# The scans of a bidirectional RWKV-7 step: from three inverse slots a chunk to one, with three units in flight

## The reference, cut to what matters

```python
xn = rms_norm(x, norm1_g) * (1.0 + sc1) + sh1
z = xn @ p['w_in']                      # r, k, v, decay and rate factors, gates, conv inputs
for each direction (forward, backward):
    def step(S, inp):
        r_t, w_t, k_t, v_t, a_t, b_t = inp
        sa = einsum('bhvk,bhk->bhv', S, a_t)
        S = S * w_t + sa[..., None] * b_t + v_t[..., None] * k_t
        return S, einsum('bhvk,bhk->bhv', S, r_t)
wkv = ys[0] + ys[1]
ln = (wkv - mean) * rsqrt(var + 64e-5) * lnx_w + lnx_b
x_a = (ln + bonuses) * (sigmoid(gl) @ g2)
out = (gate_a * (x_a @ w_pa) + gate_b * ((cb * conv(cc * ch)) @ w_pb)) @ w_o
x = x + gt1 * out;  x = x + gt2 * (relu(norm(x) @ w_ff1) ** 2 @ w_ff2)
```

## Time and profile before

| What | us |
|---|---|
| median of 3 runs | 2954.09 |
| the profiled execution, whole time | 2959.77 |
| its span | 2958.0 |
| TensorE busy in the span | 2803.4 (95%) |
| first and last `ur` copy of the scans | 1079.7 and 1753.4 |

### The profile page before, as it was taken

How to read it: one execution, slowest core, us unless ns; L and a number is a source line. 1 busy time by engine, 2 the same in 40 slices (tenths; PEclk the granted TensorE clock), 3 DMA queues, 4 the chain that set the end, 5 groups by cost and what they waited for, 6 DMA issues and landing times.

```text
span 2958.0 us, 66020 instructions
## 1 busy us (share of the span) xinstructions
PE 2803.4 (95%) x27766; PEld 2599.9 (88%) x27766; DVE 1459.0 (49%) x2957; ACT 839.9 (28%) x1684; POOL 760.4 (26%) x1005
## 2 busy tenths in 40 slices
PE   4899999999999979999999979999699999999997
PEld 2799999999999957777777769999699999999997
DVE  1364584575575536766666652442633333333333
ACT  3434234244243223333333331211411111111112
POOL 0311111111121124444444533212111111111111
PEclk8899999999999989999999999999899999999998
DMA  7323524524424434344334435212011111111101
GB/s 288 104 90 113 166 84 125 157 85 132 146 80 141 131 124 119 118 125 119 110 117 120 133 120 202 78 58 91 29 43 43 43 42 38 40 43 43 43 28 64
DMA packets 276314, 293.81 MB, mean 99 GB/s; under 512 B 76128, under 2 KB 215776, under 8 KB 275936
## 3 DMA queue, kind: packets, MB, share of 16 engines
q1 hardware_dynamic: 267104, 254.54, 28.2%
q0 software_dynamic: 7200, 28.84, 2.6%
q10 hardware_dynamic: 1760, 6.82, 0.6%
HBM read 198.76 MB, written 91.36 MB: 98 GB/s over the span
## 4 chain that ended last, share of the span: by engine, by line
PE 92%; issue 3%; DVE 2%; DMA 2%; ACT 1%; SPq 1%; POOL 0%; DVEq 0%; ACTq 0%; POOLq 0%
PE gbank L718 25%; PE inv L718 23%; PE bank L718 22%; PE ser L718 17%; PE inv L902 2%; PE bank L891 1%; DMA ring<-in_wblocks 1%; DVE xr L1578 0%; DVE xb L1985 0%; DMA xt_d<-xt_s 0%; SPq L534 0%; SPq L477 0%; POOL wsp L681 0%; DVE gmat L1746 0%; SPq L533 0%
## 5 line engine op out<-in xcount | busy, mean ns | idle before, releaser
L681 POOL TENSOR_TENSOR wsp<-ring,wsp 128x1024 fp32r<-128x1024 f32 x88 | 215.5, 2449 | 850.8 <-ACT wsp L1454 829.9
L718 PE MATMUL gbank<-xn_hi,wsp 128*128 128x384 f32 x1312 | 349.8, 340 | 19.1 <-DVE xn_lo L1942 18.2
L611 POOL TENSOR_TENSOR wsp<-ring,wsp 128x1024 fp32r<-128x1024 f32 x67 | 174.9, 2611 | 746.7 <-ACT wsp L1248 746.7
L718 PE MATMUL bank<-xn_hi,wsp 128*128 128x384 f32 x1312 | 346.9, 339 | 0.4 <-POOL wsp L681 0.4
L718 PE MATMUL inv<-xn_hi,wsp 128*128 128x384 f32 x1312 | 345.2, 338 | 0.0
L718 PEld LDWEIGHTS gbank<-xn_hi,wsp 128*128 128x128 f32 x1312 | 240.2, 189 | 24.0 <-issue 15.9
L718 PEld LDWEIGHTS bank<-xn_hi,wsp 128*128 128x128 f32 x1312 | 239.0, 188 | 2.5 <-POOL wsp L681 0.7
L718 PEld LDWEIGHTS inv<-xn_hi,wsp 128*128 128x128 f32 x1312 | 238.6, 187 | 1.8 <-POOL wsp L611 1.1
L1454 ACT ACTIVATE wsp<-ring 128x1024 fp32r<-128x1024 f32 x88 | 92.7, 1053 | 468.5 <-PE inv L718 391.9
L718 PE MATMUL ser<-xn_hi,wsp 128*128 128x384 f32 x816 | 218.9, 342 | 5.4 <-DVE xr L1578 5.4
L718 PE MATMUL bank<-xn_lo,wsp 128*128 128x384 f32 x656 | 221.3, 337 | 1.4 <-issue 1.4
(11 more groups left out here) (380 smaller groups left out, 5525.7 us busy)
## 6 DMA issues: line engine op xcount, KB each, us to landing
ring<-in_wblocks SPq DMA_DIRECT2D x195, 512.0 KB, 3.6
ub<-op_d SPq DMA_DIRECT2D x144, 256.0 KB, 2.8
op_d<-ar SPq DMA_DIRECT2D x32, 576.0 KB, 5.5
op_d<-bk SPq DMA_DIRECT2D x32, 576.0 KB, 6.2
vb<-v_d SPq DMA_DIRECT2D x144, 64.0 KB, 3.1
xt_d<-xt_s POOLq DMA_DIRECT2D x8, 576.0 KB, 3.2
x_d<-zero SPq DMA_DIRECT2D x8, 576.0 KB, 6.6
v_d<-vn SPq DMA_DIRECT2D x8, 576.0 KB, 6.8
```

Source lines behind the costliest of these rows:

```text
L611: GT(wsp[s % 2][1][:], ring[(N_ADA_RING + s) % RING][:], wsp[s % 2][0][:].bitcast(F32), ALU.subtract).then_inc(S["wsplit_lo"], 1)
L681: nc.gpsimd.tensor_tensor(wsp[b % 2][1][:], ring[(N_MIX0 + b) % RING][:], wsp[b % 2][0][:].bitcast(F32), ALU.subtract).then_inc(S["wl_ok"], 1)
L718: return nc.tensor.matmul(out, lhsT, rhs, start=start, stop=stop)
```

## The change

The scans' loop has one inverse slot a round. Round s holds the units s + 1, s + 2 and s + 3, which are at levels 5, 4 and 3, at the fixed places 0, 1, 2 (`slot`). Each step of a level is issued once for the three: three transpositions, one DVE mask, one GpSimd mask (two where the ring of 7 places wraps), three `left`, one ScalarE copy, three `right`, one DVE sum for two units (two where the ring wraps). Both Gram directions are made four rounds ahead; the transposed operands one round ahead instead of two. On TensorE the groups of one tile shape stand together. Loads go to 7 places, `gmat` to 5, `tok` to 2. The last pair's 16x16 blocks lie elsewhere (`xb`), and their 32 loads move from the dense stage to just behind the first four units' loads.

```diff
-SETS = 4
-LOADS = 6
-TOKS = 3
+SETS = 5
+LOADS = 7
+TOKS = 2
+LATE = LEVELS - FIRST
...
-        def at_level(s, i):
-            return [(s + 1, FIRST + i)] if 0 <= s + 1 < UNITS else []
+        def in_flight(s):
+            return [(v, LEVELS - v + s) for v in range(max(s + 1, 0), min(s + LATE, UNITS - 1) + 1)]
+        def slot(v, s):
+            return v - s - 1
...
# SP
-                        sp.wait_ge(S["g_out"], 32 * (p + 1))
-                        blocks_in(p)
+                        if p + 1 < PAIRS:
+                            sp.wait_ge(S["g_out"], 32 * (p + 1))
+                            blocks_in(p)
...
             pl_load(0)
             pl_load(1)
+            emptied(PAIRS - 1, "zb")
+            sp.wait_ge(S["g_out"], 32 * PAIRS)
+            blocks_in(PAIRS - 1)
             for v in range(4, LOADS):
...
# GpSimd
+            for s in range(-4, UNITS):
+                if in_flight(s):
+                    trimmed(s)
+                if there(s + 3):
+                    start_inverse(s + 3, 0)
+                    start_inverse(s + 3, 1)
+                    start_inverse(s + 3, 2)
+                if there(s + 1):
+                    triangles(s + 1)
...
# TensorE
+            for s in range(-4, UNITS):
+                p, j = divmod(s, NC)
+                inverses, serial, ahead = in_flight(s), there(s), there(s + 4)
+                if inverses:
+                    turn(s)
+                if there(s + 1):
+                    token_major(s + 1)
+                if serial:
+                    ur_state(s)
+                if ahead:
+                    gram(s + 4, 0, (0, 1, 2))
+                if serial:
+                    serial_ur(s)
+                    if j == 4:
+                        pe.wait_ge(S["ada_ok"], p + 1)
+                for x in finals(s - 1):
+                    spread(*x)
+                if inverses:
+                    left(s)
+                if serial:
+                    y_state(s)
+                if ahead:
+                    gram(s + 4, 1, (0, 1))
+                if serial:
+                    serial_u(s)
+                    if j == 2:
+                        modulation(p)
+                if inverses:
+                    right(s)
+                if ahead:
+                    gram(s + 4, 1, (2,))
+                for x in finals(s):
+                    mean(*x)
+                if serial:
+                    serial_s(s)
+                    serial_y(s)
+                    if j == 3:
+                        modulation_turned(p)
+                for x in finals(s):
+                    gate(*x)
+                    variance(*x)
...
# ScalarE, a round: deviation(s-1), y_out(s-1), tokens(s+1), ur_out, product_out, u_out,
#                   (j == 2) mrow, last_blocks(s+1), squares_of(s)
# DVE
+            for s in range(-4, UNITS):
+                p, j = divmod(s, NC)
                 if NC <= s < NC + SUB - 1:
                     substitution(PAIRS - 1, [s - NC])
+                for x in finals(s - 1):
+                    reciprocal(*x)
...
+                if there(s - 1):
+                    y_add(s - 1)
+                if in_flight(s):
+                    turned(s)
+                if there(s):
+                    carried(s)
+                if there(s + 4):
+                    gram(s + 4, 0)
+                for x in finals(s - 1):
+                    scaled(*x)
+                if in_flight(s):
+                    summed(s)
+                for x in finals(s):
+                    centred(*x)
+                if there(s):
+                    states(s)
+                    if j == NC_LAT and p + 1 < PAIRS:
+                        first_state(p + 1)
+                if there(s + 4):
+                    gram(s + 4, 1)
```

More of the change, by code:

```diff
@@ L631, in start_inverse, with trimmed @@
                     GT(lm[v % 2][part - 1][:], ltc[q][:], two(offm[:, part - 1, :]), ALU.mult).then_inc(S[f"lm{FIRST + part - 1}_ok"], 1)
-            def trimmed(s, i):
-                both, n = at_level(s, i), round_of(s, i)
+            def trimmed(s):
+                n = round_of(s)
+                pool.wait_ge(S["xt_ok"], sums(n))
                 if n:
-                    pool.wait_ge(S["xt_ok"], sums(n))
                     pool.wait_ge(S["p1_full"], n)
[L639 to L642, removed]
+                if there(s + LATE):
+                    pool.wait_ge(u_in[(s + LATE) % LOADS], 80 * ((s + LATE) // LOADS + 1))
+                parts = runs([v for v, lev in in_flight(s)])
+                for v, q in parts:
+                    x = slice(slot(v, s), slot(v, s) + q.stop - q.start)
+                    ins = GT(xtb[:, x, :, :], xt[:, q, :, :], trim[:, x, :].unsqueeze(2).to_broadcast([P, q.stop - q.start, 2, HD]), ALU.mult)
+                ins.then_inc(S["xtb_ok"], 1)
             def triangles(v):
@@ L1076, in there @@
                 return 0 <= v < UNITS
-            for s in range(-3, UNITS):
+            for s in range(-4, UNITS):
                 p, j = divmod(s, NC)
[L1080 to L1092, removed]
-                    if inverses:
-                        left(s, i)
-                    if there(s):
-                        (serial_ur, serial_u, serial_s)[i](s)
-                    if i == 0:
-                        if there(s) and j == 4:
-                            pe.wait_ge(S["ada_ok"], p + 1)
-                        for x in finals(s - 1):
-                            spread(*x)
-                    if inverses:
-                        right(s, i)
-                    if i == 0 and there(s + 2):
-                        token_major(s + 2)
-                    if i == 1:
-                        for x in finals(s):
-                            mean(*x)
-                        if there(s + 3):
-                            gram(s + 3, 0, (0, 1))
-                    if i == 2:
-                        if there(s):
-                            serial_y(s)
-                        if there(s) and j == 3:
-                            modulation_turned(p)
-                        for x in finals(s):
-                            gate(*x)
-                            variance(*x)
-                    if there(s) and j == 2 and i == 2:
-                        modulation(p)
```

198 lines of the change are left out of this document (82 added, 116 removed).

## The result

The changed kernel takes 2870.86 us (median of 4 runs, 2867.05 to 2873.18), the kernel before beside it 2956.82 (4 runs): ratio 0.9706, interval 0.9683 to 0.973. The forecast was 2903. The sign and the stage were right; the gain was 86 us instead of 51. Run again later, it gave 0.9739 (0.9715 to 0.9763).

The account below looks back on a forecast made before the run. TensorE's own queue was taken as the bound. Gains of 60 and 12.5 less losses of 10.6, 10.5 and 0.5 gave 51 us off 2959.8; less 5.7 for the median, 2903 us, range 2870 to 2940.

Parts of the forecast that it names:

- ordinary round, 70 times: Scan rounds: six fewer TensorE shape changes and shorter waits inside a level save 0.86 us a round, 60 us in all.
- waits with missing cover: TensorE waits at j = 7, j = 8 and j = 3, of 0.5, 0.5 and 0.6 us, go: 12.5 us won.
- the y add: TensorE waits 0.33 us for VectorE's `y_add` before `ur_state` in 32 rounds: 10.6 us lost.
- last pair's substitution: VectorE's step at the start of rounds 9 to 23 delays `y_add` or a mask: 10.5 us lost, 25 at most.
- last rounds, beyond an ordinary gain: The last four rounds have no Gram at all, which returns about 3 us.
- start: Moved block loads and eight Gram directions with masks before round 0 make the first serial part about 3.5 us later.
- shape is not what costs: Rival, chance 0.12: tile shape on TensorE costs nothing, only waits are gained, 5 us; total 2949.
- The slower rival: Chance 0.08: VectorE's mask of direction 1 holds TensorE 1.5 us late in all 72 rounds; total 3003.
- the price of a shape change: TensorE's queue in the scans: each change of tile shape costs 0.11 us, six fewer save 0.66 a round.
- The second reading in the forecast: By the skill's drain rule, each of six TensorE shape changes is worth 0.12 us, or 0.72 a round.
- The 0.2 for the waits of `left`: TensorE's `left` is held by the mask into `tc`; new cover saves 0.1 us for each of two levels.
- the port: VectorE's substitution multiply, with two SBUF inputs, could wait for a GpSimd instruction reading SBUF: 0.4 us a round, 6 in all.

## Why the prediction came out as it did

| step | forecast, us | measured, us |
|---|---|---|
| ordinary round, 70 times | 0.86: 60 | 1.19: 83 |
| waits with missing cover | 12.5 | 9 (0.56, 0.47 and 0.12 a pair) |
| the y add | -10.6 | -3 (0.10 a time) |
| last pair's substitution | -10.5 | -8.6 |
| last rounds, beyond an ordinary gain | 3 | 6 |
| start | -3.5 | -8.0 |
| sum in the scans and their start | 51 | 79 |
| behind the scans | 0 | 12 |

The measured column is read from round lengths; it adds to 87 for the scans where the `ur` copies say 88.6. The mechanism was right: TensorE's queue is the bound, and the shape changes are most of what moved it. The rival "shape is not what costs" fell with the Gram piece that costs 0.30 where it adds two changes and nothing where it adds none. The slower rival showed itself only where the mask was moved later. (Its price of 3003 was also summed wrongly: the 12.5 us that its own threshold counts are missing from it; with them it is about 2990.) The 12 us behind the scans were no term of the forecast and are not the change's; they took the measured time further from 2903.

*The step that failed is the price of a shape change, 0.11 us, in the first term: "Six fewer at 0.11 are 0.66".* It was the lower end of the forecast's own 0.11 to 0.14, which it read from the distance behind one group. A change is paid on both sides: the Gram piece moved shows 0.15 for each, `spread` 0.145, and the remainder for `token_major` 0.15. Six at 0.15 are 0.9, not 0.66. The second reading in the forecast, that each of the six is worth the full difference, was nearer than its row with 0.08. The 0.2 for the waits of `left` was right: in the kernel before, `left` stands 0.55 behind `y_state` (1480.58 to 1481.13), which takes 0.44 alone, and 0.54 behind a Gram piece that takes 0.44 (1483.21 to 1483.75 there), together 0.21. That leaves 1.19 - 0.9 - 0.21 = 0.08, for which the forecast had no term; 0.06 of it is `y_state` beside Gram matmuls of its own shape. The Trainium skill, TensorEngine Tiling (Array Packing), section Key Properties, says in the next line of the list that the forecast drew on that tiles operate independently; the rows at 1490.68 and 1490.70 agree. How much more the overlap could give is open, as Gram cannot start there before the mask.

*The y add was priced with durations where starts count.* VectorE and TensorE in one `y_add` round of the changed kernel:

```profile
1444.88 0.47 DVE L1805 SCALAR_TENSOR_TENSOR state<-ser,gstep,stg 128x64 f32<-128x64 f32 x2 [0.33 <-PE ser L730]
1445.27 1.21 DVE L1756 TENSOR_TENSOR gmat<-gbank,gmask 128x1024 f32<-128x1024 f32 x1
1446.40 0.15 DVE L1832 RECIPROCAL fstd<-fstd 128x2 f32<-128x2 f32 x1
1446.47 0.40 DVE L1816 TENSOR_TENSOR yf<-ser,yf 128x256 f32<-128x256 f32 x1
```
```profile
1445.92 0.55 PE L916 MATMUL inv<-ident,xt 128*128 128x128 f32 x3
1446.93 0.46 PE L730 MATMUL ser<-state,ub 64*64 64x64 f32 x16
```

`states` begins 1.04 before the transpositions; the forecast had 1.05. But state, mask and reciprocal follow each other after 0.39, 1.13 and 0.07, since an instruction's row overlaps the next one's by 0.08. The forecast added 0.45, 1.23 and 0.15. So `ur_state` starts at 1.01 instead of 1.3, and loses 0.10 instead of 0.33.

*The substitution* was right in the five rounds with `y_add` (6.5 forecast, 6.6 measured: 1.26, 1.34, 2.09, 1.05, 0.88) and too dear in the ten others (4.0 against 1.8). No run isolated the port that the forecast took into its upper bound of 25; 8.6 came back with the step moved.

*The waits with missing cover* were 9 instead of 12.5, mostly because at j = 8 a new wait of 0.27 for the mask stands where the old one of 0.5 went.

*The start* was too cheap. The masks of the changed kernel on VectorE:

```profile
1061.19 1.23 DVE L1756 TENSOR_TENSOR gmat<-gbank,gmask 128x1024 f32<-128x1024 f32 x1
1064.52 1.23 DVE L1756 TENSOR_TENSOR gmat<-gbank,gmask 128x1024 f32<-128x1024 f32 x1 [2.11 <-PE gbank L730]
...
1084.16 1.23 DVE L1756 TENSOR_TENSOR gmat<-gbank,gmask 128x1024 f32<-128x1024 f32 x1
```

The relay of Gram direction and mask was there as forecast, but the first five steps take 3.3 to 3.8 us each and not 1.23 + 1.4, as a direction takes 2.03 at the low clock; the next three take 2.7 to 3.0. Up to the first `ur` copy there are nine masks where the kernel before has six, and from the first mask to that copy it was 26.5 (1061.19 to 1087.7) against 19.6 before (1060.13 to 1079.7). The first mask itself came 1.1 later, which is within its spread from one profile to the next. So 6.9 of the 8.0 are the longer relay. The loads of units 4 to 6, which the forecast feared, never held it. In front of the first mask stands, in both kernels, the load for the first state.

## What to carry to other kernels

When TensorE's queue is the bound, count the changes of tile shape in the order of the queue, and price one by moving a group and reading the starts on both sides of it: here about 0.15 us each. When moving a group costs something with no shape changed, ask first what it covered: look at the start of the next group against the end of what it depends on, since the modelled end of a matmul can hide a wait of 0.2 us from the lists. Sum a chain on one engine from start to start, since durations in the rows overlap; and before comparing whole times, look at a stretch that no edit touches.

## What was not expected of the hardware

The last stage, the same code in all kernels, ran at one of three paces in an execution, at a granted clock of 1.00, with TensorE at 100% and no waits. The kernel before and the changed one, in the windows:

```profile
2300.00:2500.00 200.00, 200.00 (x1134) 200.00 (x1133) 69.31 (x133) 28.71 (x40) 38.37 (x16) 1.00 0.12 39
```
```profile
2300.00:2500.00 200.00, 200.00 (x1156) 200.00 (x1155) 71.08 (x136) 28.79 (x41) 38.61 (x17) 1.00 0.13 42
```

1134, 1147 or 1156 matmuls in 200 us are 176.4, 174.4 or 173.0 ns from one to the next. The changed kernel showed 1156 in one profile and 1147 in another, and so did the one with the late substitution; the one with the late first state showed 1134 and 1147. So it doesn't go with the kernel, and 2% of some 1190 us is as much as the runs of one kernel differ. What sets the pace was not tried. The 12 us that the profiled pair gained behind the scans are of this kind, and 80 of the 86 are the change's own by the rounds; with the two comparisons at 0.9706 and 0.9739, it is worth 78 to 86 us.

The granted clock falls not only in long idle stretches. At the start of the scans TensorE stands still for 0.8 to 1.2 us of every 3.3 to 3.8 while a mask is made. In the kernel with the extra matmuls the clock was 1.00 up to 1062, and then 0.74 over 1062 to 1088 with these gaps alone; the changed kernel, which came into them at the low clock, had 0.65. In the rounds that follow, without such gaps, it was 1.00.
